# Order of the expert rows: a flat table of shares, the norm of y for one block on ScalarE, and the transposes of y behind the last gate product

## What is computed

```python
y = group_rmsnorm(y * jax.nn.silu(z.astype(jnp.float32)), norm_g, SSD_N_GROUPS)   # 8 groups of 256
return y.astype(xs.dtype) @ w_out
...
merged = (g[..., :D_MODEL] * y_ssd + g[..., D_MODEL:] * y_sc).astype(x.dtype)
h = h + merged @ w_o[l]
```

```python
q = (xb @ w_q).reshape(PEER_BLOCK, PEER_HEADS, 2, PEER_HALF)
s = jnp.einsum('thjd,hjkd->thjk', q, sub_keys).astype(jnp.float32)
sv, si = lax.top_k(s, PEER_TOPK)
cand = sv[:, :, 0, :, None] + sv[:, :, 1, None, :]
cs, ci = lax.top_k(cand.reshape(PEER_BLOCK, PEER_HEADS, PEER_TOPK * PEER_TOPK), PEER_TOPK)
...
u = expert_u[eidx]
v = expert_v[eidx]
act = jax.nn.gelu(jnp.einsum('td,thkd->thk', xb, u).astype(jnp.float32), approximate=False)
return jnp.einsum('thk,thkd->td', (g * act).astype(v.dtype), v)
```

## Time and profile before

| | us |
|---|---|
| median of 3 runs | 2426.34 (2426.01 to 2430.4) |
| the profiled execution | 2426.01 |
| its span, first to last instruction | 2424.2 |
| TensorE busy | 2170.6 (90%) |
| VectorE busy | 1499.9 (62%) |
| ScalarE busy | 639.7 (26%) |
| GpSimd busy | 1017.3 (42%) |

### The profile page before, as it was taken

The page is one execution under the profiler, slowest core; times in us unless marked ns, Lnnn a source line. Parts: engine busy times, 40 slices in busy tenths (PEclk is TensorE's granted clock), DMA queues, the critical chain, the costliest instruction groups (busy, mean ns, idle before and its releaser), DMA issues.

```text
span 2424.2 us, 29421 instructions
## 1 busy us (share of the span) xinstructions
PE 2170.6 (90%) x10898; PEld 1522.4 (63%) x10898; DVE 1499.9 (62%) x3475; ACT 639.7 (26%) x1802; POOL 1017.3 (42%) x1028
## 2 busy tenths in 40 slices
PE   8999999999999899889797673399889999999898
PEld 7999886666666788776551263133377555447595
DVE  3442159999999737975829289810177768875210
ACT  6673235555555413000100010010121000002310
POOL 0000003555565411463657666667635657760000
PEclk9999999999999999999899986699998999999999
DMA  6666746999999896999999999999998999997384
GB/s 237 217 222 224 272 185 230 380 389 376 361 373 351 317 390 256 406 409 412 410 394 410 409 380 410 410 376 410 411 383 335 412 412 412 411 412 307 113 335 160
DMA packets 191839, 831.37 MB, mean 343 GB/s; under 512 B 21440, under 2 KB 21696, under 8 KB 159952
## 3 DMA queue, kind: packets, MB, share of 16 engines
q0 software_dynamic: 147456, 536.94, 56.7%
q1 hardware_dynamic: 43664, 290.46, 31.6%
q10 hardware_dynamic: 576, 2.10, 0.2%
HBM read 827.31 MB, written 2.10 MB: 342 GB/s over the span
## 4 chain that ended last, share of the span: by engine, by line
PE 49%; DVE 20%; DMA 18%; POOL 5%; issue 4%; ACT 3%; DVEq 0%; ACTq 0%; POOLq 0%
PE ps L1117 49%; DVE rows L2503 10%; DMA rows<-in_pv,eidx 7%; DMA rows<-in_pu,eidx 5%; DMA rows<-in_pv,eidxT 5%; POOL rows L1089 5%; DMA wr<-in_wgate 1%; DVE h L2527 1%; DVE arena L2125 1%; DVE ps L2527 1%; ACT arena L1605 0%; DVE rows L2039 0%; DVE wb L2361 0%; DVE rows L2037 0%; PE ps L1233 0%
## 5 line engine op out<-in xcount | busy, mean ns | idle before, releaser
L1089 POOL DMA_INDIRECT rows<-in_pu,eidx x512 | 485.4, 948 | 846.8 <-DVE arena L2125 364.7
L1117 PE MATMUL ps<-arena,wr 128*128 128x128 f32 (+4 forms) x3968 | 762.7, 351 | 19.7 <-DVE arena L2228 8.5
L1117 PEld LDWEIGHTS ps<-arena,wr 128*128 128x128 f32 x3968 | 600.9, 193 | 162.7 <-issue 21.3
L2503 DVE CUSTOM_DVE_ANT_0 rows<-rows,ps 128x1024 f32<-128x1024 f32 x512 | 601.6, 1216 | 46.0 <-DMA rows<-in_pu,eidx 41.6
L1089 POOL DMA_INDIRECT rows<-in_pv,eidx x256 | 287.8, 1124 | 191.7 <-DVE h L2527 106.6
L1117 PE MATMUL ps<-hT,wr 128*128 128x128 f32 (+2 forms) x1600 | 353.3, 382 | 7.0 <-DVE xx L2384 5.5
L1117 PEld LDWEIGHTS ps<-hT,wr 128*128 128x128 f32 x1600 | 256.3, 195 | 100.5 <-issue 8.0
L1089 POOL DMA_INDIRECT rows<-in_pv,eidxT x256 | 243.9, 953 | 127.5 <-issue 64.0
L1117 PE MATMUL ps<-rows,wz 128*32 128x512 f32 x1024 | 213.0, 614 | 50.4 <-DMA rows<-in_pv,eidxT 48.9
L1117 PE MATMUL ps<-wr,arena 128*128 128x256 f32 (+2 forms) x704 | 179.5, 410 | 0.0
L2527 DVE SCALAR_TENSOR_TENSOR h<-rows,wgt,h 128x1024 f32<-128x1024 f32 x132 | 169.0, 1280 | 10.1 <-DMA rows<-in_pv,eidx 9.1
(11 more groups left out here) (369 smaller groups left out, 2257.3 us busy)
## 6 DMA issues: line engine op xcount, KB each, us to landing
wr<-in_wg SPq DMA_DIRECT2D x48, 1024.0 KB, 7.0
wr<-in_wgu SPq DMA_DIRECT2D x33, 1024.0 KB, 8.3
wr<-in_wgate SPq DMA_DIRECT2D x24, 1024.0 KB, 7.9
wr<-in_wso SPq DMA_DIRECT2D x24, 1024.0 KB, 8.0
wr<-in_wq SPq DMA_DIRECT2D x16, 1152.0 KB, 8.1
wr<-in_wsc SPq DMA_DIRECT2D x16, 1024.0 KB, 5.7
wr<-in_wqku SPq DMA_DIRECT2D x15, 1024.0 KB, 8.1
wr<-in_wdn SPq DMA_DIRECT2D x14, 1024.0 KB, 7.9
```

Of the source, the lines that this page charges most:

```text
L1089: e.indirect_dma_start(ring[slot_of[i]], None, A[table], bass.IndirectOffsetOnAxis(ap=index[:, t, k:k + 1], axis=0)).then_inc(gathered[slo ...
L1117: return e.matmul(o, l, r, start=start, stop=stop, skip_group_check=True)
L2503: e.tensor_tensor_reduce(row, row, wide[:], 1.0, 0.0, MUL, ADD, dots[:, k:k + 1]).then_inc(*dve.up(*u))
```

## The change

Five edits:

- `QUOTA` has one number per stage instead of a list, and `make_plan` spreads it evenly over the stage's cost. The totals per stage are nearly the same: of the stages that differ by more than 4 rows of 0.5 MB, the stage behind the scan of block 1 (`late`, 1) goes from 8 to 0, `feed` 0 part 0 from 47 to 39, part 1 from 15 to 23, the first half of the down projection from 36 to 24, and the second half from 36 to 44.
- `CY` goes from 2.0 to 4.2, and one step of the sums of block 2 is taken ahead of the merge with the choice of block 1.
- In `plan_sum` all gate products that come ahead of the transposes stand ahead of them; before, the last of them stood behind.
- The norm of y for block 2 is no longer planned within the sums of block 1, but behind the second gate product of block 2, and
- its multiplications are done by ScalarE, 16 copies with a scale; VectorE still makes the mean and the reciprocal root.

```diff
-CY = 2.0
+CY = 4.2
...
-QUOTA = {('top', 0): (0,), ('mixer', 1, 0): (0,), ('mixer', 1, 1): (7, 11, 10), ('mixer', 1, 2): (8, 8, 11, 9), ('mixer', 1, 3): (12, 5, 10, 6), ('mixer', 1, 4): (11, 14, 5), ('mixer', 1, 5): (10, 9, 11), ('mixer', 1, 6): (17, 0, 9, 8), ('mixer', 1, 7): (9, 11, 7), ('mixer', 1, 8): (3, 8), ('late', 1): (8,), ('sum', 1): (12,), ('query', 1): (6,), ('top', 1): (0,), ('late', 2): (0, 14), ('sum', 2): (10, 10, 7, 9, 12, 18, 0, 17), ('query', 2): (15, 11, 7, 11, 19, 1, 9, 16), ('top', 2): (0,), ('top', 3): (0, 9, 12, 15, 12, 0, 15, 10), ('attend', 0): (18, 28, 0, 18, 0, 12, 27, 32), ('heads', 0): (5, 0, 22, 12, 12), ('wout', 0): (16, 9, 15, 2, 10, 9), ('attend', 2): (7, 7, 7), ('heads', 2): (3, 4, 4), ('wout', 2): (6, 0, 4), ('feed', 0): (9,), ('feed', 0, 0): (17, 10, 13, 7), ('feed', 0, 1): (3, 4, 8), ('feed', 0, 2): (9, 14, 0, 21, 7, 0), ('feed', 0, 3): (10, 2, 5), ('down', 0, 0): (13, 16, 10), ('down', 0, 1): (23, 15, 20, 10, 30, 17, 0, 29)}
+QUOTA = {('query', 2): 90, ('top', 3): 74, ('attend', 0): 140, ('heads', 0): 47, ('wout', 0): 53, ('attend', 2): 21, ('heads', 2): 11, ('wout', 2): 9, ('feed', 0): 10, ('feed', 0, 0): 39, ('feed', 0, 1): 23, ('feed', 0, 2): 55, ('down', 0, 0): 25, ('down', 0, 1): 125, ('top', 2): 0, ('query', 1): 6, ('feed', 0, 3): 16, ('top', 0): 3, ('mixer', 1, 0): 0, ('mixer', 1, 1): 28, ('mixer', 1, 2): 36, ('mixer', 1, 3): 33, ('mixer', 1, 4): 26, ('mixer', 1, 5): 31, ('mixer', 1, 6): 35, ('mixer', 1, 7): 29, ('mixer', 1, 8): 16, ('late', 1): 0, ('sum', 1): 12, ('late', 2): 15, ('sum', 2): 79, ('top', 1): 0, ('defer', 2): 20}
...
-    for j in range(AHEAD_GATES[q] - 1):
+    for j in range(AHEAD_GATES[q]):
         yield from gate_products(j)
+        if q == 2:
+            yield "gated"
     if q == 2:
-        yield "gated"
+        for part in range(2):
+            pl.add("ynorm", q, part, v=nt * vc((1792, 256)[part]))
     for i in range(4 * nt):
         pl.take(("yturn", q, i), "lo", ("act", "yturn", q, i))
         pl.add("yturn", q, i, p=0.48)
         yield True
-    yield from gate_products(AHEAD_GATES[q] - 1)
...
-        if q == 1 and j in (2, 4):
-            pl.add("ynorm", 2, j // 4, v=2 * vc((1792, 256)[j // 4]))
...
+        yield next(sums[2])
         yield from merge(pl, (choose[1], 0.001), (sums[2], CY))
...
-        parts = QUOTA.get(stage, (0,))
-        begun = spent.get(stage, 0.0)
-        spent[stage] = begun + cost * len(parts) / max(whole[stage], 1e-9)
-        due += sum(n * max(0.0, min(spent[stage], i + 1) - max(begun, i)) for i, n in enumerate(parts))
+        due += QUOTA.get(stage, 0) * cost / max(whole[stage], 1e-9)
...
-                    w.wait_ge(*dve.at("ynorm", q, 1 if per * (i + 1) > 14 else 0))
+                    w.wait_ge(*(act if q == 2 else dve).at("ynorm", q, 1 if per * (i + 1) > 14 else 0))
...
+                    if q == 2:
+                        nt, nr, off, first = columns_of(q)
+                        w.wait_ge(*dve.at("rsqrt", "y", q, part))
+                        for c in range(nt):
+                            for g in range(7 * part, 7 + part):
+                                yv = yh_of(scan_of(q), first + c, g)
+                                e.activation(yv, yv, ACT.Copy, scale=S[q]["rs0"][:, c, g:g + 1]
+                                             ).then_inc(*act.up("ynorm", q, part))
...
-                    for c in range(nt):
+                    for c in range(nt if q < 2 else 0):
```

More of the change, by code:

```diff
@@ L763, in more @@
         return x is not None
-    due, spent = 0.0, {}
+    due = 0.0
     for r, stage, cost in costs(pl):
```

## The result

The changed kernel took 2457.01 us (median of 4 runs, 2454.41 to 2466.84), the kernel before 2428.37 us (4 runs, 2426.01 to 2431.01). The ratio is 1.0125, with a 95% interval of 1.0109 to 1.0141: 28.6 us by the medians, 30 us by the ratio. The profiled execution of the changed kernel took 2461.35 us (span 2459.5), 35.3 us more than the one of before, so what is read from the two traces adds up to 5 to 7 us more than the medians show.

What follows compares the result with a forecast made beforehand. TensorE was taken to set the pace up to about 950 us, bytes from 952 to about 2190 us, then TensorE alone. Terms 5.7 + 13 + 2 = +20.7 us on 2426 us gave 2447 us, range 2431 to 2463 us.

Steps and rivals of the forecast that it cites:

- Term 1: Transposes of y, blocks 0 and 1: TensorE waits for ScalarE's copies, 3.1 and 2.6 us, +5.7 us before 952 us.
- Term 2: Norm of block 2 in the decode: VectorE loses about 8 us, 6 us of it waiting behind ScalarE's fourteen copies.
- Term 3: Choice of block 1, 952 to 1026 us: fewer gathers ahead, 5.1 MB missing on the DMA engines, +13 us (0 to 19).
- the 9.2 us: Choice of block 1: last piece out earlier by this much, 17 us of dot products saved against 8 us of norm and row-0 wait.
- Term 4: Flat table elsewhere, in mixer and feed-forward stages: rows shift by 0 to 12 per stage, +2 us together.
- rival C: Flat table costs its bound: ten us more in feed-forward, up to 4 in the mixer, 2459 us; chance 0.18.
- Rival A: Missing bytes are made up in later soft places of the DMA engines, the 13 us vanish: 2434 us; chance 0.17.
- Rival B: VectorE is the true limit from 952 to 1036 us, the earlier choice makes it faster: 2422.5 us; chance 0.07.
- The sign that the tail behind 2190 us keeps its length: End of the kernel: everything shifts by about 20 us, but 2190 us to the end of the span stays 234 us.

Runs made afterwards that it cites:

- g2: Kernel before with only the last gate product moved ahead of the transposes of y: 1.0058 of before.
- g1: Kernel before with only the norm of y for block 2 moved later and multiplied by ScalarE: 2443.0 us against 2425.6 us, 1.0071 of before.
- g4: Kernel before with only the flat QUOTA table, where TensorE runs freely: 2441.58 us, 1.0068 of before.
- e2: Changed kernel with the norm of y for block 2 put back on VectorE in the sums of block 1: 2521.8 us, 0.9978 of before.
- e1: Changed kernel with CY back at 2.0 and without the early first step of the sums of block 2: 2528.6 us, 0.9998 of before.
- f1: Kernel before, unchanged, traced again in a series where TensorE stalls: 2541.61 us in one execution.
- f3: Kernel before with only CY at 4.2 and the early first step, in a series where TensorE stalls: 1.0108 of before.
- f2: Kernel before with only the flat QUOTA table, in a series where TensorE stalls: 0.9918 of before, 22.7 us faster.

## Why the prediction was right, and where its parts were not

The forecast was 2447 us in a range of 2431 to 2463 us, and 2457.01 us were measured: inside the range, 10 us above the forecast. How late the same matmuls of TensorE start, against the first trace of before (medians over the matmuls that start there in the 25 us from the place named, which is in the time of before):

| at us | changed | g2 transposes | g1 norm | g4 flat table |
|---|---|---|---|---|
| 300 | 1.2 | 4.9 | -3.7 | -4.4 |
| 675 | 1.0 | 1.7 | -2.5 | -2.5 |
| 775 | 4.7 | 0.8 | -1.7 | 0.1 |
| 925 | 7.7 | 3.9 | 0.2 | -0.5 |
| 1100 | 21.3 | 9.2 | 19.3 | -1.0 |
| 1350 | 24.2 | 7.7 | 17.2 | 2.4 |
| 1750 | 26.7 | 7.6 | 16.6 | 5.6 |
| 2050 | 25.5 | 6.4 | 16.7 | 5.5 |
| 2125 | 28.6 | 8.5 | 18.6 | 7.6 |
| 2250 | 33.0 | 6.2 | 13.9 | 9.5 |
| 2400 | 35.3 | 6.2 | 16.2 | 11.9 |

Steps of 2 to 3 us in single traces are spells of the lower clock that fall elsewhere: the changed kernel has one of 7 us at 2111 us (before one of 4 us in the same work), one of 14.5 us at 2237 us (before 7 us) and one of 7 us at 2330 us (before none; granted clock 0.83 over 2325 to 2345 us, against 1.00 in the same work before), some 7 us of its 35.3 in all; against that all four traces have a head start of 1.4 to 2.5 us on the first trace of before at 675 us, beyond the 3.1 us of the first transposes, whose source was not followed. What is left in the changed kernel is 30 us, as the medians and the ratio have it: 5.6 us of waits at the transposes, 3.7 us in the mixer (675 to 775 us), 13.6 us in the stretch of the choice (925 to 1100 us), 4.2 us from there to 2050 us, and 2.8 us at the handover of tile 3.

In these traces the last values of the three parts alone add up to 34.3 us, against 35.3 us for all. By the medians they do not: 17.4 (g1), 13.0 (g2) and 15.9 us (g4) are 46 us, and the whole change costs 28.6 us. So either parts of it overlap, or CY gives some of it back, or the medians of four runs each carry several us that are not the kernels'. Which of these it is stays open, and the split of the 30 us by parts rests on the traces.

- **Term 1, the transposes: right.** 5.7 us forecast, 3.10 + 2.53 us of waits measured, 6.2 us left at the end of the trace when done alone (13 us by its medians).
- **Term 2, the wait of VectorE: right in place and size** (6 us forecast, 5.83 measured; 8.9 us of VectorE's time instead of 8). What it left out is that TensorE stops for the same copies, 12.10 us here and 16.91 us in g1, where this makes the second wait of VectorE. VectorE waited 0.28 us for the first root, so the table load of 1.28 us lay beside the dot products. The Trainium skill (ScalarE: Activation LUTs, What ACT_TABLE_LOAD costs) has about 2.7 us with the drain; nothing of the drain is seen in this trace, where ScalarE's next activation starts 0.02 us behind the load, and the 1.4 us more that it would have made did not come. Sixteen multiplications on ScalarE delayed VectorE more than its own 3.96 us for them. The Trainium skill (ScalarE: Activation LUTs, Rules for kernel authors) advises VectorE for a multiplication; e2 and g1 agree with the advice, though the page gives the speed per element as its reason and these runs show a queue.
- **Term 3, the stretch of the choice: the size right, the reason wrong.** 13 us forecast, 17.2 us measured as idle of the DMA engines (20.0 less 2.8), 13.6 us as delay of TensorE. Choice, ring, gathers and bytes came out as worked out (the bracket behind the 9.2 us does not add up: 17 less 8 less the wait for row 0 is about 7; 8.4 us were measured). But I put the loss down to the 15 dot products fewer ahead of the opening. e1 has 32 of them and loses as much; g1 has 33 and loses as much with CY untouched. So that the size fits is in good part luck. Up to the 43rd gather VectorE has the same work in whichever order, and GpSimd makes up for late gathers once 13 slots are open. What counts is what is added to VectorE's time (the norm alone: 14.1 us longer than the first trace of before and 11.5 to 11.7 us longer than g2 and g4, of which 8 were foreseen and 6.4 are the second wait) and what weights are taken away (CY: 6.8 us alone). The two do not add: in the changed kernel, with both, the second wait is covered, and putting CY back gives nothing.
- **Term 4, the flat table: the failed size.** +2 us forecast; 10.7 us in the trace of the changed kernel (3.7 + 4.2 + 2.8), 11.9 us at the end of g4's and 16 us by g4's medians. In both traces some 3 to 4 us are lost in the mixer (a new wait of 2.64 to 3.09 us), 4 to 7 us by small idle pieces between 1100 and 1750 us, the rest at the handover of tile 3 (and, in g4's 11.9 us, in spells of the lower clock). That the pieces in the changed kernel are the table's is read from g4, which has them in the same places with nothing else changed. I had both places at the end and in the mixer in rival C, but bounded the middle at nothing, since the DMA engines are full there on average. Their soft spots are where a table of numbers acts.
- **Rival A** (made up later) fell: 19.3 us at 1100 us are still 16.7 at 2050 (g1), 21.3 are 25.5 (changed). **Rival B** fell: the choice came out 8.4 us earlier in its own time, and nothing was faster. **Rival C** (2459 us) is nearer to the 2457 us than the forecast of 2447 us; its term of 14 us was right within some 3 us in size, not in place: no 10 us are lost in the feed-forward stages.

With the 13.6 us of delay for term 3, the forecast's 20.7 us become 30 by the flat table alone: 2 us forecast, 10.7 us in the trace. The sign that the tail behind 2190 us keeps its length did not come: it grew by some 10 us, 2.8 us of it the handover and the rest the low-clock spells.

Not tried: CY alone with TensorE running freely, so its share of the 30 us is not shown. Open: what makes the lists the slower ones when TensorE stalls. The DMA engines of f1 and f3 idle 13 to 17 us more than those of f2 in each of two places, about 1650 to 1775 and 1985 to 2110 us; which wait there turns over was not followed.

## What to carry to other kernels

Where an engine is nearly full, count what is added to its time and what it newly waits for; how its old work is ordered mattered less here than it looked, since GpSimd could catch up behind it. Moving an operation to an idle engine pays only if nobody stands behind it there, and that means every engine that reads the result: here 4 us of VectorE's work became 5.8 to 12 us of VectorE's waiting and 12 to 17 us of TensorE's. And a table that is tuned on one occasion says little on another: the same two kernels had ratios of 1.0125 and 0.998.

## What the runs showed of the hardware

TensorE can be slow in a way that the two levels of the granted clock don't tell. The waits of TensorE with no releaser, first of f2, then of g4, the same kernel on the same chip:

```profile
PE ps L1114 <- issue: 91.2, 72, 7.9
```

```profile
PE ps L1114 <- issue: 5.7, 2, 5.2
```

f2 in one of these stretches:

```profile
1503.82 0.17 PE L1114 MATMUL ps<-lf,con 128*128 128x8 f32 x1 [0.18 <-issue]
1505.21 0.17 PE L1114 MATMUL ps<-lf,con 128*128 128x8 f32 x1 [1.22 <-issue]
...
1512.23 0.17 PE L1114 MATMUL ps<-lf,con 128*128 128x8 f32 x1 [2.65 <-issue]
...
1519.93 0.59 PE L1114 MATMUL ps<-hT,wr 128*128 128x256 f32 x1 [2.21 <-issue]
```

In the 40 us from 1500 us TensorE did 38 matmuls, with a granted clock of 0.57 on average; eight columns take about as long as 256 from start to start (1.4 to 2.8 us). f2 took 78 us longer than g4 in all. Single records may be missing from a trace, but VectorE and the DMA engines are late behind these stretches too, so the time is real. The Trainium skill (TensorE: Matmul & The Clock Gate, Seeing it yourself) warns that the clock records of this chip can be unreliable; the starts of the matmuls are the better witness, and they agree with the warning.

What sets these stretches off was not studied.
